# Two moves in a one-core decoder step: the first MoE gathers no longer held back, and ten convolution taps placed in later attention cycles

## The reference, cut to what matters

```
u = h @ w_in                                  # q, k, v (8 heads x 64) and two 512-wide halves for the convolution
att = stick_breaking(q, k, v)                 # sigmoid(-z), reversed running product over keys, times sigmoid(z)
y[t] = sum over tap 0..30 of glu[t - 30 + tap] * conv_w[tap] + conv_b      # per channel, 512 channels
cv = silu(layernorm(y))
x = x + gate1 * (concat(att, cv) @ w_out)
h2 = modulate(rmsnorm(x)); two experts of 16 for each token, inside one group of 4
act = silu(h2 @ w_gate[e]) * (h2 @ w_up[e]) * p[e];   x = x + gate2 * sum over e of act @ w_down[e]
```

## Time and profile before

| what | value |
|---|---|
| runs | 1239.95, 1241.55, 1242.26 us; median 1241.55 |
| the profiled execution's own time | 1239.21 us |
| its span (first to last instruction) | 1237.5 us |
| TensorE busy | 93% of the span |
| VectorE busy | 49% |
| ScalarE, GpSimd busy | 27%, 21% |
| mean granted TensorE clock | 0.976 |
| DMA | 253.37 MB, 205 GB/s on average |

### The profile page before, as it was taken

The page is one execution under the profiler, slowest core; times in us unless marked ns, Lnnn a source line. Parts: engine busy times, 40 slices in busy tenths (PEclk is TensorE's granted clock), DMA queues, the critical chain, the costliest instruction groups (busy, mean ns, idle before and its releaser), DMA issues. The chain is left out here.

```text
span 1237.5 us, 19314 instructions
## 1 busy us (share of the span) xinstructions
PE 1153.4 (93%) x6769; PEld 538.4 (44%) x6769; DVE 601.9 (49%) x1161; ACT 337.3 (27%) x713; POOL 255.1 (21%) x312
## 2 busy tenths in 40 slices
PE   6999999999989999998999966899999999999996
PEld 3444444444446666665444433233333333333332
DVE  0010867786779999897965357111211211211212
ACT  2132221222038888887212221000000000000000
POOL 2011101111049600000100000223232233232322
PEclk9999999999999999999999986999999999999999
DMA  9943333332247465645833246996689877976663
GB/s 360 334 137 102 103 103 107 100 86 84 90 157 259 138 201 173 208 137 207 317 115 110 87 150 239 348 396 238 235 281 330 313 271 257 369 240 245 219 214 131
DMA packets 115859, 253.37 MB, mean 205 GB/s; under 512 B 15054, under 2 KB 29518, under 8 KB 114760
## 3 DMA queue, kind: packets, MB, share of 16 engines
q1 hardware_dynamic: 94241, 208.42, 48.2%
q0 software_dynamic: 17568, 39.35, 9.0%
q10 hardware_dynamic: 3984, 4.72, 1.1%
HBM read 399.77 MB, written 39.22 MB: 355 GB/s over the span
## 5 line engine op out<-in xcount | busy, mean ns | idle before, releaser
L1785 PE MATMUL bank<-big,mid 128*64 128x512 f32 x1232 | 282.8, 600 | 7.4 <-DMA big<-in_w_up_dram 5.9
L1462 PE MATMUL bank<-big 128*128 128x512 f32 x560 | 249.2, 598 | 0.1
L1462 PEld LDWEIGHTS bank<-big 128*128 128x128 f32 x560 | 103.6, 190 | 131.3 <-issue 131.3
L1785 PEld LDWEIGHTS bank<-big,mid 128*64 128x64 f32 x1232 | 87.0, 138 | 168.2 <-issue 166.5
L1958 DVE SCALAR_TENSOR_TENSOR cvT<-low,cw,cvT 128x256 f32<-128x256 f32 x360 | 158.7, 518 | 0.0
L1799 PE MATMUL bank<-big,mid 128*64 128x512 f32 x608 | 133.7, 592 | 0.7 <-DMA big<-in_w_down_dram 0.7
L2063 DVE TENSOR_TENSOR_SCAN big<-big 128x513 f32<-128x513 f32 (+4 forms) x96 | 90.2, 978 | 8.1 <-ACT big L1091 8.1
L2485 DVE TENSOR_TENSOR xt<-xt,bank 128x512 f32<-128x512 f32 x20 | 13.8, 688 | 146.3 <-ACT xt L1259 131.8
L1799 PEld LDWEIGHTS bank<-big,mid 128*64 128x64 f32 x608 | 44.0, 137 | 87.4 <-issue 87.4
L2504 DVE TENSOR_TENSOR mid<-bank,low 128x512 f32<-128x512 f32 x38 | 24.5, 686 | 112.9 <-PE bank L1799 92.5
L800 POOL TENSOR_TENSOR st<-st,mhalf 128x16 f32<-128x16 f32 (+1 forms) x9 | 25.2, 2800 | 254.3 <-DVE st L1989 245.5
(11 more groups left out here) (341 smaller groups left out, 1323.3 us busy)
## 6 DMA issues: line engine op xcount, KB each, us to landing
big<-in_w_gate_dram SPq DMA_DIRECT2D x42, 2048.0 KB
big<-in_w_up_dram SPq DMA_DIRECT2D x41, 2048.0 KB
big<-in_w_down_dram SPq DMA_DIRECT2D x41, 2048.0 KB
low<-in_w_ada_dram SPq DMA_DIRECT2D x32, 512.0 KB, 4.1
low<-in_cache_v_dram SPq DMA_DIRECT2D x64, 256.0 KB
big<-in_w_in_dram SPq DMA_DIRECT2D x8, 1280.0 KB, 17.3
xt<-in_x_prompt_dram SPq DMA_DIRECT2D x16, 512.0 KB, 4.8
mid<-in_w_ada_dram SPq DMA_DIRECT2D x8, 1024.0 KB, 13.9
```

The lines of the kernel that those rows point to most:

```text
L1462: mm = pe.matmul(bank[:, 4 if cc == 2 else cc, :], hT[:, s, k, :], w_in_sb[:, k, cc * 512:(cc + 1) * 512], start=(k == 0), stop=(k == KD - 1))
L1785: mm = pe.matmul(bank[half, 2 * s + w, :], xgT[:, s, k, half], moving, start=(k == 0), stop=(k == KD - 1))
```

## The change: what it does

It takes one wait out of GpSimd's list, and moves two VectorE instructions a cycle from attention's cycles 0 to 4 to its cycles 9 to 13. No instruction is added or removed, no data or buffer changes.

```diff
             fetch_x(0)
             fetch_x(1)
             pool.wait_ge(S["tok_ready"], 2)
-            pool.wait_ge(S["u_mm"], 1)
             for landed, n0 in zip(x1_st, X1_ST0):
                 pool.wait_ge(landed, n0 + 16 * (NT // 3))
             gather_out(0, 0, 1, 16)
...
-            LATE_TAP = 26
+            LATE_TAP, LATE_FROM = 26, 9
...
-                if cy < CW - LATE_TAP:
-                    conv_taps(NTP // 2 - 2, (2, 3), LATE_TAP + cy, LATE_TAP + cy + 1)
+                if LATE_FROM <= cy < LATE_FROM + CW - LATE_TAP:
+                    tap = LATE_TAP + cy - LATE_FROM
+                    conv_taps(NTP // 2 - 2, (2, 3), tap, tap + 1)
                 for tap in range(TAPS_BY[cy], TAPS_BY[cy + 1]):
                     conv_tap(tap)
```

## The result

The changed kernel took 1234.04 us (median of 1235.05, 1233.76, 1232.49 and 1234.32) against 1241.9 us of the kernel before on the same chip (1239.95, 1241.55, 1242.26, 1245.57): ratio 0.9947, 95% interval 0.9928 to 0.9965. Forecast were 1238.8 us and a range of 1236.2 to 1242.0. The sign was right, the gain was more than twice as large, and the time lies outside the range.

A forecast was written before the change was run, and what follows sets the result against it. TensorE was taken as the bound, waiting on VectorE in attention and on DMA transfers at the experts' start. 0.36 us (taps) plus 2.4 (gathers) gave 2.8 off 1241.55: 1238.8 us, range 1236.2 to 1242.0.

The forecast's parts named there:

- Taps, cycle 5: Attention, cycle 5 to 6: with the taps gone, VectorE's L2089 is no longer late for TensorE; 14.09 becomes 13.73, gain 0.36 us.
- Taps, cycles 9 to 14: Attention: 4.7 us of VectorE work returns in cycles 9 to 13, covered by 7.39 us idle; TensorE's cycles as long as before.
- DMA holes: Start of the experts: early gathers fill 2.4 us of unused DMA time in 772 to 775 and 779 to 783.
- Issue times: GpSimd at the start of the experts: without the wait, everything starts 13 us earlier, copy at 766.9, L894 at 775.8.
- Gate wait: TensorE before gate 1, first expert steps: the wait for gate weights grows from 0.86 to about 2.2 us.
- The larger ends of the two holes: Start of the experts: upper end of the filled DMA time, both holes filled whole, 3.1 us.
- TensorE is held there by the DMAs, as before, 2.4 us earlier.: Down 1 and the up weights behind it: weights land 2.4 us earlier, TensorE still waits for them, 2.4 us stay won.
- Tile 4: Experts: its gather is next to be late, landing 827.0 against 827.5 wanted, after 3.4 us in hand before; it just holds.
- the slower one: Start of the experts: gathers delay gate weights by all 5.2 us, tile 4 late, 1243.5 us; slower by either way 0.12.
- The rival through the clock: Gate 1: 2.2 us wait drops TensorE's clock, down 0 ends at 798.3, tile 4 late; 1239.8 us, chance 0.2.
- The median: Whole kernel: the forecast subtracts 2.8 us from a median of 1241.55 us, giving 1238.8 us.

The follow-up runs named there:

- n_chain_y7: Kernel before, with the last gather of token tile 1's outputs and the x gather behind it held until the first half of down 1; 1241.09 us, ratio 1.0001.
- h_x4_held: Kernel before, with tile 4's gather and all behind it in GpSimd's queue held until up of step 2 is done; 1248.42 us, ratio 1.0068.
- a_wait_only: Kernel before with only the held wait on u_mm taken out, taps still in cycles 0 to 4; 1236.28 us, ratio 0.9971.
- k_out_held: Changed kernel with the early output gather and the x gather swapped in GpSimd's queue, x early, outputs held; 1235.88 us, ratio 0.9957.
- p_out_held_y7: As k_out_held, but GpSimd's next pair of gathers also held until the first half of down 1; 1237.72 us, ratio 0.9975.
- f_taps_twice: Kernel before with each of the ten taps executed twice in cycles 0 to 4, so the output differs; 1238.84 us, ratio 0.9996.

## Why the prediction was wrong

**Taps, cycle 5: right to a hundredth, and too narrow.** 14.09 to 13.72 us, and no wait for VectorE. The step that failed is "That 0.36 us is all I find of VectorE on the path". It is all of it in an execution whose clock had fallen two cycles earlier. The row for that was quoted: a granted clock of 0.91 beside 18.10 us of VectorE's work in 18.27. The 18.10 were read and the 0.91 was not. With the clock up, the same backlog costs a wait of 1.8 us, in one of two profiles half clock after it, and with early taps the clock falls in cycle 7 as well in some executions. The term of 0.36 us measures 2.4, standard error 0.5. The fact that VectorE never idles was the better row to count by: a queue that is always full sets the time whatever the other engine's wait says.

**Taps, cycles 9 to 14: right.** They cost nothing; cycle 9 to 10 takes 13.71 us after, 13.73 before. Cycles 5 to 9 do as well.

**DMA holes: right in kind, nearly in size.** Issue times: copy forecast 766.9, after has 764.79, and its turn of tile 0 is 2.0 us earlier; L894 forecast 775.8, is 772.98. Filled time forecast 2.4, found 1.9 by the bytes up to down 1. (One slip of the working had no consequence: weights that landed at 800.2 land at 797.8 when they come 2.4 us earlier, and not at 797.5.) Gate wait forecast 2.2, is 2.34, and 1.9 to 3.0 in the other runs without the hold. The larger ends of the two holes (3.1 us) were in the range.

**The missing term: "TensorE is held there by the DMAs, as before, 2.4 us earlier."** This is the step that failed for the hold: 3.9 us were measured for its 2.4, where the taps' step missed by 2.0. It took the landing as the sum of bytes ahead, which is right, and took the bytes as unchanged, which is wrong; and TensorE is still held by the DMAs at down 1, 2.9 us earlier, but no longer at step 2. The contradiction stands in the forecast itself: it has the scatter of step 0 come 0.45 us later, and so the gathers behind it, while the weights come 2.4 us earlier. Two transfers that move by different amounts can change their order. Here the gathers came 2.3 to 3.4 us later and the weights 2.9 us and more earlier, counted from the turn of tile 0: the gate rows fell behind the down weights (1.0 us) and the next two gathers behind the up weights of step 2 (1.0 us). n_chain_y7 and h_x4_held show the second by itself, as the wait of 0.78 us that goes; the first is read from the bytes alone. Sum for the hold: 1.9 + 1.0 + 1.0 = 3.9 in the stage, and 3.9 us in the time (a_wait_only).

The Trainium skill, page "DMA: Bandwidth & Descriptors", section "Queues, rings and completion order", has each DMA engine take turns over the queues with work. The prediction used that against the gate weights only; the queue rows of k_out_held (0.41 MB beside 0.39, then 0.50 beside 0.30) show the same beside later loads. The profile's packets agree with equal turns: where both queues run through the window they are near equal in number (137 and 146, and 141 and 147 in the earlier trace rows), and only the bytes are not, since a packet of the gathers holds 3.6 KB and one of the loads 2.0.

**Tile 4: wrong, without consequence.** The L875 at 818.61 fetches x for tile 4, and tile 4 is turned in step 3, at 852.41 in before and 846.43 in after; 829.89 is the turn of tile 3. There were 26 us in hand, not 3.4. Two rivals, the clock one and the slower one, took their price from that wait. GpSimd's true limit there is VectorE's combine, as h_x4_held shows at 8 us.

**The rival through the clock: its first half came true.** After 2.34 us of waiting the clock did fall (matmuls of 1.06 us instead of 0.59 at 781.80, granted clock 0.57 in 781 to 785), and down 0 ended 3.4 us later, counted from the turn of tile 0, where the rival had 3.0. It cost nothing in the end, since down 1 waits for its weights anyway (1.19 us); it even kept the gathers back while the weights passed. The clock fell after each of the six gate waits of 2.34 to 3.04 us in the profiles with early output gathers, and not after those of 1.90 and 1.91 in k_out_held and p_out_held_y7. The rival's second half, a late tile 4, did not come.

**The median.** 1238.8 was counted from a median of three, which is 1.2 us above the mean of 131. From 1240.4 the forecast's 2.8 would have read 1237.6; the gain would have been wrong all the same.

## What to carry to other kernels

When a change makes one queue's transfers earlier and leaves another's where they are, list for every later load what stands ahead of it before and after: an order that flips is worth up to all the bytes of the transfer that is passed, as long as the engine still waits for the load; here 2.0 us, as much as the idle time that was filled. Count an engine that never idles by its own work, not by the wait of the engine that it feeds, and look at the granted clock of the very window that the wait is read from, since a slow stretch of the one hides the lateness of the other. And a gain in a stage is only a gain if the later steps' loads keep up: p_out_held_y7 was 3.1 us ahead of k_out_held at step 2 and gave back 5.4.

## What the runs showed of the hardware that was not expected

- In attention the clock falls in the same few places: the scores that take 1.8 to 2.08 us instead of 1.13 come in cycles 3, 7 or 11, in some executions and not in others of the same kernel (f_taps_twice left out, cycle 3 in 12 of 17 profiles). Ahead of the one in cycle 3 TensorE waits 1.19 us for ScalarE in every one of these profiles, so the wait alone does not decide it. What goes with it is how attention began: from the first 512-wide scores to those of cycle 1 it is 19.11 to 19.49 us in the 12, and 19.94 to 19.96 in the 5 in which the clock stayed up, as the half clock at the start lasted longer there (360 to 376: granted clock 0.79 in before, 0.68 in after). In f_taps_twice, with VectorE later still, it was 19.22 and the clock stayed up.
- Gathers beside a stream of weights took 52 to 65% of the DMA engines. In after, from 779 to 781, they had all of it: 0.78 MB, 100.0%, the weights 0.01 MB. That is not the gathers alone: in before, with no gather there, the weights' queue moved nothing from 780 to 781 either. Its data came back in 781 to 782 in both, with the up weights issued at 780.10 in before and at 778.24 in after.
- Executions of one kernel scatter by 1.75 us (standard deviation, 131 executions on three chips from 1235.8 to 1244.7). A part worth 2 us needs ten or more executions to be seen, and one profile shows one of several cases.
